# A decoder trunk with a 32-expert layer on one core: row order, biases and weight homes changed

## The reference, cut to what matters

```python
h2 = rms_norm(x, norm2_g) * (1.0 + sc2) + sh2
logits = h2 @ w_router + b_router               # 32 experts
top_val, top_idx = lax.top_k(logits, 4);  wts = softmax(top_val)
# for each expert e, over the tokens that chose it:
gu = xb @ w_gu[e] + b_gu[e]                     # (1024 x 1024), bias of 1024
gt, up = gu[:, :512], gu[:, 512:]
gt = minimum(gt, 7.0);  up = clip(up, -7.0, 7.0)
act = gt * sigmoid(1.702 * gt) * (up + 1.0)
y = act @ w_down[e] + b_down[e]                 # (512 x 1024)
x = x + g2 * sum_of(wts * y);  out = rms_norm(x, final_g)
```

## Time and profile before

| what | us |
|---|---|
| median of 3 runs | 937.23 (936.38 to 937.92) |
| the profiled execution | 932.74 |
| its span | 931.0 |
| PE busy | 895.7 (96%) |
| PEld busy | 525.3 (56%) |
| DVE busy | 454.4 (49%) |
| ACT busy | 180.2 (19%) |
| POOL busy | 250.0 (27%) |
| DMA, mean over the span | 305 GB/s, 283.75 MB |

### The profile page before, as it was taken

The page is one execution under the profiler, slowest core; times in us unless marked ns, Lnnn a source line. Parts: engine busy times, 40 slices in busy tenths (PEclk is TensorE's granted clock), DMA queues, the critical chain, the costliest instruction groups (busy, mean ns, idle before and its releaser), DMA issues.

```text
span 931.0 us, 22683 instructions
## 1 busy us (share of the span) xinstructions
PE 895.7 (96%) x10115; PEld 525.3 (56%) x10115; DVE 454.4 (49%) x946; ACT 180.2 (19%) x361; POOL 250.0 (27%) x248
## 2 busy tenths in 40 slices
PE   3999999999999998989999999999999999999994
PEld 2676756766788755755545454544545454544551
DVE  0389967544633556754352534344352534344355
ACT  6344454544322414100000000000000000000012
POOL 2333952202400003223223131323223131323102
PEclk9999999999999999999999999999999999999998
DMA  9937554305422967679999999999999999999965
GB/s 322 366 130 271 181 173 157 123 1 198 175 96 79 408 259 293 257 301 354 375 407 390 407 399 402 404 399 407 394 409 395 409 397 407 404 402 408 391 246 195
DMA packets 64124, 283.75 MB, mean 305 GB/s; under 512 B 7428, under 2 KB 9052, under 8 KB 39448
## 3 DMA queue, kind: packets, MB, share of 16 engines
q1 hardware_dynamic: 53528, 257.93, 69.8%
q0 software_dynamic: 10496, 24.32, 9.3%
HBM read 271.83 MB, written 18.50 MB: 312 GB/s over the span
## 4 chain that ended last, share of the span: by engine, by line
PE 84%; DVE 9%; ACT 3%; DMA 2%; issue 1%; SPq 0%; DVEq 0%; ACTq 0%; POOLq 0%
PE ps L1859 36%; PE ps L1578 16%; PE ps L1882 12%; PE ps L1872 6%; PE ps L1813 2%; DVE small L1157 2%; DVE top L1156 2%; PE ps L1632 2%; PE ps L1718 2%; PE ps L1853 2%; PE ps L1599 1%; DMA moe_rows<-X 1%; PE ps L1733 1%; DVE small L1142 1%; DMA X<-in_x_dram 1%
## 5 line engine op out<-in xcount | busy, mean ns | idle before, releaser
L1354 DVE TENSOR_SCALAR mix<-ps 128x384 f32<-128x384 f32 x32 | 17.9, 558 | 280.1 <-ACT attn L1019 280.1
L753 POOL DMA_INDIRECT moe_rows<-mix,idx x31 | 45.9, 1482 | 345.6 <-DVE mix L1412 345.6
L1578 PE MATMUL ps<-h_hi,wb_hl 128*128 128x512 f32 x384 | 125.5, 400 | 0.0
L1019 ACT ACTIVATE attn<-ps 128x384 f32<-128x384 f32 x32 | 15.7, 491 | 493.2 <-PE ps L1859 493.2
L747 POOL DMA_INDIRECT apad<-h_rows,idx x93 | 97.3, 1046 | 50.6 <-issue 27.7
L1578 PEld LDWEIGHTS ps<-h_hi,wb_hl 128*128 128x128 f32 x384 | 72.1, 188 | 20.8 <-issue 3.9
L1859 PE MATMUL ps<-ring,mix 128*32 128x256 f32 x1440 | 80.0, 379 | 0.0
L1859 PE MATMUL ps<-ring,uvp 128*32 128x256 f32 x1344 | 76.3, 383 | 0.0
L1578 PE MATMUL ps<-h_lo,wb_hl 128*128 128x512 f32 x192 | 74.8, 390 | 0.0
L1404 DVE SCALAR_TENSOR_TENSOR mix<-ps,WC,attn 32x256 f32<-32x256 f32 x128 | 61.6, 481 | 3.8 <-PE ps L1872 1.4
L1859 PEld LDWEIGHTS ps<-ring,mix 128*32 128x32 f32 x1440 | 43.0, 110 | 33.1
(11 more groups left out here) (312 smaller groups left out, 1346.7 us busy)
## 6 DMA issues: line engine op xcount, KB each, us to landing
ring<-in_w_gu_dram SPq DMA_DIRECT2D x58, 1024.0 KB, 23.8
ring<-in_w_down_dram SPq DMA_DIRECT2D x30, 1024.0 KB, 25.7
ring<-in_w_ada_dram SPq DMA_DIRECT2D x12, 2048.0 KB, 11.2
area_b<-in_w_gu_dram SPq DMA_DIRECT2D x17, 1024.0 KB, 18.9
hT<-in_w_gu_dram SPq DMA_DIRECT2D x17, 1024.0 KB, 22.9
area_a<-in_w_gu_dram SPq DMA_DIRECT2D x15, 1024.0 KB, 23.7
X<-in_w_gu_dram SPq DMA_DIRECT2D x14, 1024.0 KB, 26.1
ring<-in_w_in_dram SPq DMA_DIRECT2D x6, 2048.0 KB, 9.1
```

Of the source, the lines that this page charges most:

```text
L753: pool.indirect_dma_start(out=y_dram, in_=Y[0:slots, b, :], in_offset=None, out_offset=bass.IndirectOffsetOnAxis(ap=which, axis=0), bounds ...
L1578: last = mm(out_, a, b, start=(n == 0 and start_), stop=(n == len(pairs) - 1))
```

## The change

1. Natural row order. h2 keeps the model's column order; `h2_rows` adds with inputs in order and without the wait for y_begun in chunks 2 and 3, chunk 2 lives in uvp and not in X, and TensorE reads a contraction block with a step of eight elements (`h2_block`). GpSimd's copy for the quarter rows reads with the step too.
2. VectorE biases. The twelve bias matmuls, `b3`, `sel3` and GpSimd's seven operations for them are gone. Four DMAs bring b_gu in another order, one VectorE transpose makes `bias_cols`; for each expert VectorE turns a column into a row (`bias_rows`), adds it to the up result in PSUM with the sum in SBUF (`biased`, 128x768), and clamp, sigmoid and product read that. `up(e)` on TensorE waits for `biased_ok` of the expert before it, in place of `av_ok`; the sigmoid waits for `biased_ok`.
3. Own index step. The first group's rows get their own `quarter_rows` in bank 3 directly after `places(0)`, which stands after six of the eight blocks of the first gather. `rows(1)` stands ahead of `gated(0)`.
4. Homes. PRE is 19. `small` becomes home 12 and is loaded as soon as the A jobs and the row write are done; x1's scratch moves from small to apad. attn[2048:4096] becomes a home, since the one-hots move to mix, and the scale row g2b takes n2b's place, loaded after the h2 writes.

```diff
-PRE = 18
+PRE = 19
-        h2 = [X[:, ch, :] for ch in range(C - 1)] + [apad_flat[:, PG * (PAD + T) - D:PG * (PAD + T)]]
+        h2 = [X[:, 0, :], X[:, 1, :], uvp[:, :, :].rearrange("p a t -> p (a t)"),
+              apad_flat[:, PG * (PAD + T) - D:PG * (PAD + T)]]
+        h2_block = [t.rearrange("p (q k) -> p k q", k=KD) for t in h2]
-        g2b = attn[:, 3072:4096]
+        g2b = n2b
...
-        homes = ([...] + [small[:, :], latent[:, :]]
+        homes = ([...] + [attn[:, 2048:4096], latent[:, :]]
                  + [last_pair[:, i * PAIR:(i + 1) * PAIR] for i in range(2)])
-        kept = [i for i in range(PRE) if i != 2 * len(pairs)]
+        homes.insert(12, small[:, :])
+        kept = [i for i in range(PRE) if i != 12]
...
             load_up(2, 1, 11)
+            sp.wait_ge(by_vec, emptied[number["A", KD - 1]])
+            sp.wait_ge(row_out, 32)
+            load_up(2, 2, 12)
             used(NFP - 1)
-            load_up(2, 2, 12)
             load_up(2, 3, 13)
-            sp.wait_ge(by_vec, emptied[number["out", 2 * C - 1]])
             load_down(1, 0, 14)
+            sp.wait_ge(h2_ok, C)
+            load_down(1, 1, 15)
             sp.wait_ge(job_done, number["rt", 0] + 1)
             sp.wait_ge(h2_out[0], 8 * C)
-            load_down(1, 1, 15)
+            load_up(3, 0, 16)
             sp.wait_ge(tx_done, 1)
...
-            load_up(3, 0, 16)
             load_up(3, 1, 17)
+            load_up(3, 2, 18)
...
+            def bias_rows(cols, done):
+                v.transpose(brow.rearrange("p (m f) -> p m f", m=8),
+                            cols.rearrange("p (m s) -> p m s", s=1).broadcast_to([P, 8, SB])).then_inc(done, 1)
             def h2_rows(ch):
...
-                v.tensor_tensor(h2[ch].rearrange("p (k q) -> p k q", k=KD), by_k(natural), by_k(sh2b),
-                                ALU.add).then_inc(h2_ok, 1)
+                v.tensor_tensor(h2[ch], scaled, sh2b, ALU.add).then_inc(h2_ok, 1)
...
-            def activate(up_done, th_done, gate, prod, done, n):
+            def activate(up_done, with_bias, th_done, mid, done, n):
                 dve.wait_ge(*up_done)
+                v.tensor_tensor(biased, ps[:, 0:SG, 0:2 * P], brow.rearrange("p (g n) -> p g n", g=1)
+                                .broadcast_to([P, SG, 2 * P]), ALU.add).then_inc(with_bias, 1)
...
-            for g in (2, 3, *LATE_GROUPS[0]):
+            for g in (3, *LATE_GROUPS[0]):
                 one_hot(g)
+            rows(1)
             gated(0)
-            rows(1)
...
-                for g in range(SG):
-                    for j in range(4):
-                        mm(ps[SB * j:SB * (j + 1), g, 0:2 * P], bias.broadcast_to([3 * NE, SB]), b3_of[:, j, :, :],
-                           start=True, stop=False, tile_position=(0, SB * j))
...
-                        last = nc.tensor.transpose(b_[:, k * P:(k + 1) * P], h2[ch][:, at:at + P], ident[:, :])
+                        last = nc.tensor.transpose(b_[:, k * P:(k + 1) * P], h2_block[ch][:, 4 * half + k, :], ident[:, :])
...
+                if k == 5:
+                    places(0)
             last.then_inc(tx_done, 1)
-            places(0)
+            quarter_rows(3, 0, OHE)
...
-                    pe.wait_ge(av_ok, e)
+                    pe.wait_ge(biased_ok, e)
```

More of the change, by code:

```diff
@@ L191, in trunk @@
         natural = uvp[:, :, :].rearrange("p a t -> p (a t)")
-        first = natural[:, 0:C * slots].rearrange("p (c s) -> p c s", c=C)
+        first = mix[:, 3072:3072 + C * slots].rearrange("p (c s) -> p c s", c=C)
         lgT = T3[:, 2, :]
@@ L391, in trunk @@
         last_pair = X[:, :, :].rearrange("p c d -> p (c d)")
-        homes = ([t[:, i * PAIR:(i + 1) * PAIR] for t in pairs for i in range(2)] + [small[:, :], latent[:, :]]
+        homes = ([t[:, i * PAIR:(i + 1) * PAIR] for t in pairs for i in range(2)] + [attn[:, 2048:4096], latent[:, :]]
                  + [last_pair[:, i * PAIR:(i + 1) * PAIR] for i in range(2)])
-        kept = [i for i in range(PRE) if i != 2 * len(pairs)]
+        homes.insert(12, small[:, :])
+        kept = [i for i in range(PRE) if i != 12]
         home_of = list(range(PRE)) + [kept[i % len(kept)] for i in range(NE * PER - PRE)]
@@ L549, in _ @@
             for e in range(3, NE):
-                for q in range(2 if e == 3 else 0, 4):
+                for q in range(3 if e == 3 else 0, 4):
                     refill_up(e, q)
@@ L627, in _ @@
                                              base=-part * NE, pattern=[[-1, NE]], channel_multiplier=1))
-            link(nc.gpsimd.memset(sel3[:, :], 0.0))
-            for part in range(3):
-                link(nc.gpsimd.affine_select(out=sel3[:, :], in_=sel3[:, :], compare_op=ALU.not_equal, fill=1.0,
-                                             base=-part * NE, pattern=[[-1, NE]], channel_multiplier=1))
             for g in range(PG):
@@ L1461, in expert @@
                 if e == 3:
-                    dve.wait_ge(rep_ok, 2)
-                    quarter_rows(2 * OHE, NE - 2 * OHE)
+                    dve.wait_ge(rep_ok, 3)
+                    quarter_rows(5, 2 * OHE, NE - 2 * OHE)
                 gated(e)
                 weighted(e - 1, 1 - b, reused)
-            dve.wait_ge(rep_ok, 1)
-            quarter_rows(0, 2 * OHE)
-            for g in (2, 3, *LATE_GROUPS[0]):
+            one_hot(2)
+            dve.wait_ge(rep_ok, 2)
+            quarter_rows(5, OHE, OHE)
+            for g in (3, *LATE_GROUPS[0]):
                 one_hot(g)
+            rows(1)
             gated(0)
-            rows(1)
             dve.wait_ge(g2_in, 16)
@@ L1847, in _, with up_all @@
             chain(b_[:, C * NE:(C + 1) * NE], [(onesb[:, :], maskh[:, k, :]) for k in range(C)], job_done)
-            def up_all(b, bias, arrived, done, between={}):
-                for g in range(SG):
-                    for j in range(4):
-                        mm(ps[SB * j:SB * (j + 1), g, 0:2 * P], bias.broadcast_to([3 * NE, SB]), b3_of[:, j, :, :],
-                           start=True, stop=False, tile_position=(0, SB * j))
+            def up_all(b, arrived, done, between={}):
                 for k in range(KD):
@@ L1904, in arrived @@
                     return up_view(up_no(e, k // 2))
-                up_all(e % 2, sel3[:, e:e + 1], arrived, half_used, between)
+                up_all(e % 2, arrived, half_used, between)
             def down(e, at=3):
@@ L1950, in _ @@
                 for ch in range(C):
-                    last = mm(ps[:, 4 + k // 4, (k % 4) * P:(k % 4) * P + slots], h2[ch][:, k * P:(k + 1) * P], first[:, ch, :],
+                    last = mm(ps[:, 4 + k // 4, (k % 4) * P:(k % 4) * P + slots], h2_block[ch][:, k, :], first[:, ch, :],
                               start=(ch == 0), stop=(ch == C - 1))
+                if k == 5:
+                    places(0)
             last.then_inc(tx_done, 1)
-            places(0)
+            quarter_rows(3, 0, OHE)
             start("ix", 1)
@@ L1965, in expert @@
                 if e == 0:
-                    up(0, {0: lambda: quarter_rows(0, 2 * OHE), 2: lambda: places(2), 5: lambda: places(3)})
+                    up(0, {0: lambda: quarter_rows(5, OHE, OHE), 2: lambda: places(2), 5: lambda: places(3)})
                 elif e == 3:
-                    up(3, {1: lambda: quarter_rows(2 * OHE, NE - 2 * OHE)})
+                    up(3, {1: lambda: quarter_rows(5, 2 * OHE, NE - 2 * OHE)})
                 else:
```

131 lines of the change are left out of this document (65 added, 66 removed).

## The result

| what | before | after |
|---|---|---|
| median of 8 runs each, us | 936.75 (934.65 to 937.92) | 942.30 (940.49 to 945.34) |
| the profiled execution, us | 932.74 | 942.58 |
| its span, us | 931.0 | 940.8 |

The changed kernel is slower: ratio 1.0066, 95% interval 1.0051 to 1.0080, some 5.5 us. The forecast was 929.0 us and the range ended at 937.5; both missed. The two profiled executions differ by 9.8 us, because the one of before lies 4 us under its median, and under all eight of its runs.

The account below looks back on a forecast made before the run. Weight transfers, 2.90 us each, were taken to bound the kernel; their stream ending 2.9 + 5.5 us earlier, less 1.2, plus slack of 0.5 to 1.1, took 8.2 off 937.2: 929.0 us, 8-in-10 range 924.5 to 937.5.

Parts of the forecast that it names:

- What bounds the kernel: Over the experts: weight transfers, 17.3 us an expert against TensorE's 16.1, set the end; a faster TensorE alone gains nothing there.
- The other side of that edit: TensorE's h2 loads at a step of eight, 72 passes in router transposes and first gather: +1.2 us, from 0 to +10.
- the slower rival: Stepped h2 loads on TensorE cost beyond double, gain used up at 228 ns a load: 939 to 945 us, chance 0.08.
- Natural row order: VectorE's h2 adds before the first gather, in order, take 1.23 us instead of 2.04: gather starts 1.6 us earlier.
- The 19th home: One more weight transfer done beforehand, into small at about 333 us: -2.9 us at the end, 0.3 us allowed for y_begun.
- The wait of 2.46 us: TensorE's wait before up(1) goes: weight matmuls at 397.3 instead of 401.69, clock 1.1 us, first tile release 5.5 us earlier.
- Bias by VectorE: In each expert twelve bias matmuls go, 10.5 us of TensorE over 31 experts, nothing at the end; VectorE add 0.95, transpose 0.42.
- places(0) inside the gather: 16 small matmuls in the first gather take 0.8 us; expert 0 starts +0.1 us, first gathers at 383.4 instead of 387.3.

Follow-up runs that it names:

- e10: The changed kernel with h2 stored k outer, the transfer into small issued late and half of each down's wide contraction left out: 925.22 us, before 935.72 there.
- e6: The kernel before with a tail of matmuls, adds and copies at several steps behind its last use of TensorE: 1029.27 us, where before takes 972.55.
- e5_again: The changed kernel with h2 stored k outer again and the transfer into small issued after the output matmuls: 930.02 us against 935.72 before, ratio 0.9948.
- e3: The changed kernel with the transfer into small issued behind the wait for the output matmuls: 969.56 us against 972.16 before, ratio 0.9972.
- a0_after: The changed kernel run again without an edit, on a chip at 972 us: 971.93 us against 972.55 before, ratio 0.9992.

## Why the prediction was wrong

*What bounds the kernel.* Right, on the chips at 936 us. TensorE's 0.30 us an expert came back as waits in the last six experts, and e10 shows the bound by itself. Its 17.1 us an expert confirm the 17.3 of the sum (six times 2.90 is 17.4). On the chips at 972 us TensorE is the bound, and there the removed bias matmuls do count (8.7 us from up(4) to up(31), 468.2 against 459.5).

*"The other side of that edit".* This is the step that failed. I put a stepped load at 1.0 ns a value, "+1.2 us", from a range of 0 to +10 us. Measured: 238 ns a pass, so 64 x (238 - 112) = 8.1 us in the gather alone, 6.9 more than the whole term. The eight transposes of the 72 passes cost nothing. The mechanism was in the text as the slower rival, and 238 ns is above its point of 228 ns; I gave it 0.08 because VectorE's add with two stepped inputs is only 1.6 times as long. e6 shows why this speaks for nothing: one stream costs as much as two, and VectorE's instruction in order is slower for a value (1.2 ns) than TensorE's load (0.87 ns), so that the same 1.9 ns a value is a factor of 1.6 there and of 2.1 here. For the gather the value should have been carried over as ns a value, 2.0, which was my own upper bound (255 ns). Put into the sum, the measured term alone makes it 929.0 + 6.9 = 935.9 us, still inside the range; the steps below took the time out of it.

*What that step drew with it.* The clock fell to 0.50 during the gather. Of what is not a stepped load, the first half of `places` took 0.6 us more than in e5_again, the rest of the index step 0.7 us more (394.28 to 396.09, where e5_again has 384.40 to 385.51), and the first 72 passes of up(0) 6.30 us where e5_again takes 4.32, 2.0 us more. I had counted a gain of 1.1 us from the clock.

*Natural row order.* Forecast 1.6 us earlier at the first gather; it is 2.1 us later, with the longer wait of the next paragraph in it. The size of the adds was right (1.23 us). The sum has no term for GpSimd's copy, and I hadn't asked what it does to VectorE: it holds L1277 until it ends, 0.9 to 1.0 us in each of three chunks. The page "SBUF — State Buffer", section "SBUF: two separate sides" of the Trainium skill says that GpSimd and a VectorE operation with two SBUF inputs share a port pair and one blocks the other fully. The traces agree: L1277 ends 1.09 to 1.10 us after the copy in all three chunks.

*The 19th home.* "I allow 0.3 us for a later y_begun": between the two profiled executions it is 2.7 us (4.46 against 1.80), and e3 gives 2.4 us back. The wait of before isn't constant, though: e6 has 3.5 us, and against that the 4.8 us of a0_after on the same chip are 1.3 more. The price of one transfer, 2.9 us, fits the stream's rate; that a home is worth it isn't shown.

*The wait of 2.46 us* and *Bias by VectorE.* Right: up(1) follows up(0)'s work without a wait, 10.5 us long (forecast 10.4 for a later one), the bias add takes 0.96 us and the transpose 0.40 (forecast 0.95 and 0.42), and biased_ok is never waited for.

*places(0) inside the gather.* It cost 1.3 us at 388.99 instead of 0.8, at the low clock.

Put together at up(1): forecast 397.3, measured 412.3. Of these 15.0 us the step holds about 7, the later start 3.7, the low clock 3.3; the remaining 1 us I didn't separate. With h2 in the old order and the transfer late (e5_again), up(1) began at 399.7 and the kernel took 930.0, near the 929.0 that I forecast for the change as it was. That is partly luck: the kernel before took 935.7 there, so the gain is 5.7 us where the sum gave 8.2. The parts of the sum on the index step, the wait before up(1) and the bias were sound; the stepped load was the largest miss, and the late start and the clock came on top. The rows of the two new VectorE instructions, after:

```profile
L1348 DVE TENSOR_TENSOR mix<-ps,mix 128x768 f32<-128x768 f32 x6 | 5.7, 958 | 45.7 <-PE ps L1862 45.7
...
L1268 DVE STREAM_TRANSPOSE mix<-maskb 128x256 f32<-128x256 f32 x7 | 2.8, 402 | 0.0
```

## What to carry to other kernels

A layout edit moves the cost of a step from one reader to the next: count every reader, and bound each by the time for a value of a stepped stream (here 1.9 ns for float32, on VectorE and in the gather's matmuls), not by the ratio that another engine shows. A bound is what that is: the eight transposes paid nothing for the same step. Put the step where it is hidden; before 64 loads that are the pace of their stage it is dear. Ask too what a longer copy on GpSimd and an earlier transfer do to the engine beside them. Where the sum hangs on one price that no row shows and whose upper bound turns the sign, the chance belongs to that price, and not to the row that is pleasant.
